# First two projection units piece by piece over the tokens, transposes of x between their k steps, in a retention and attention layer

## The reference, cut to what matters

```python
def _rms_norm(x, g):
    x32 = x.astype(jnp.float32)
    y = x32 * lax.rsqrt(jnp.mean(x32 * x32, axis=-1, keepdims=True) + RMS_EPS)
    return (y * g.astype(jnp.float32)).astype(x.dtype)

hn = _rms_norm(x, norm_mix[l])
proj = hn @ w_in
rq, rk, rv, rg, aq, ak, av, gr, ga = jnp.split(proj, ...)
```

## Time and profile before

| what | us |
|---|---|
| median of three runs | 1802.99 |
| the profiled execution | 1802.53 |
| its span, first to last instruction | 1800.6 |
| TensorE busy | 1769.1 |
| POOL, VectorE, ScalarE busy | 882.4, 765.8, 473.3 |

### The profile page before, as it was taken

One profiled execution on the slowest core, in us unless ns is written; L12 is line 12 of the kernel. 1 busy time (PEld: TensorE's weight loads), 2 busy tenths in 40 slices (PEclk: granted clock), 3 DMA queues, 4 the chain that ended last, 5 costly groups with the idle time before them and its releaser, 6 DMA issues.

```text
span 1800.6 us, 29667 instructions
## 1 busy us (share of the span) xinstructions
PE 1769.1 (98%) x12218; PEld 1729.1 (96%) x12218; DVE 765.8 (43%) x813; ACT 473.3 (26%) x879; POOL 882.4 (49%) x450
## 2 busy tenths in 40 slices
PE   7999999999999999999899998999999999999998
PEld 6999999999999999999899998999999999999998
DVE  4143444443222213314845678455444444632313
ACT  5001010100411125447101125433333333201003
POOL 3323232324333333332336448988888887344550
PEclk9999999999999999999999999999999999999999
DMA  6212121224222252452834342222222221723122
GB/s 241 83 57 64 57 63 58 66 92 152 82 84 90 76 177 88 150 180 75 236 86 144 126 141 83 71 70 70 92 95 70 93 70 50 291 91 122 53 63 95
DMA packets 172694, 186.64 MB, mean 104 GB/s; under 512 B 7353, under 2 KB 149937, under 8 KB 172633
## 3 DMA queue, kind: packets, MB, share of 16 engines
q1 hardware_dynamic: 143088, 136.87, 23.7%
q10 hardware_dynamic: 29545, 48.90, 7.9%
HBM read 131.99 MB, written 53.76 MB: 103 GB/s over the span
## 4 chain that ended last, share of the span: by engine, by line
PE 92%; DVE 4%; ACT 1%; issue 1%; POOL 1%; DMA 0%; ACTq 0%; DVEq 0%; SPq 0%
PE unit_ps L896 55%; PE pair_ps L1232 23%; PE unit_ps L1302 4%; PE task_banks L1081 2%; PE task_banks L1058 1%; PE task_banks L1068 1%; PE task_banks L1008 1%; PE task_banks L985 1%; PE task_banks L992 1%; PE task_banks L994 1%; PE task_banks L1043 0%; PE task_banks L980 0%; PE task_banks L1016 0%; PE task_banks L965 0%; DVE parts L2184 0%
## 5 line engine op out<-in xcount | busy, mean ns | idle before, releaser
L896 PE MATMUL unit_ps<-a_hi,w_part 128*128 128x344 f32 x3552 | 716.5, 327 | 4.7 <-DVE a_lo L1860 3.7
L896 PEld LDWEIGHTS unit_ps<-a_hi,w_part 128*128 128x128 f32 x3552 | 578.5, 189 | 14.8 <-issue 10.6
L776 POOL TENSOR_TENSOR w_part<-w_raw,consts 128x1024 fp32r<-128x1024 f32 (+1 forms) x89 | 212.2, 2384 | 735.1 <-PE unit_ps L896 705.4
L896 PE MATMUL unit_ps<-a_lo,w_part 128*128 128x344 f32 x1776 | 377.3, 321 | 0.0
L896 PEld LDWEIGHTS unit_ps<-a_lo,w_part 128*128 128x128 f32 x1776 | 300.6, 189 | 0.0
L778 POOL TENSOR_TENSOR w_part<-w_raw,w_part 128x1024 fp32r<-128x1024 f32 (+1 forms) x91 | 240.5, 2643 | 7.0
L1232 PE MATMUL pair_ps<-a_hi,slots_a 128*128 128x258 f32 x1056 | 178.4, 283 | 3.4 <-DVE a_lo L2256 1.5
L1232 PEld LDWEIGHTS pair_ps<-a_hi,slots_a 128*128 128x128 f32 x1056 | 148.8, 190 | 4.5 <-DVE a_lo L2256 1.8
L1835 DVE TENSOR_TENSOR stage<-unit_ps,rstd 128x1032 f32<-128x1032 f32 x42 | 51.7, 1231 | 206.4 <-PE unit_ps L896 206.4
L896 PE MATMUL unit_ps<-b_hi,w_part 128*128 128x344 f32 x720 | 133.4, 320 | 0.0
L896 PEld LDWEIGHTS unit_ps<-b_hi,w_part 128*128 128x128 f32 x720 | 117.0, 188 | 0.3 <-DVE gate_a L2218 0.3
(11 more groups left out here) (266 smaller groups left out, 2677.6 us busy)
## 6 DMA issues: line engine op xcount, KB each, us to landing
w_raw<-in_w_in SPq DMA_DIRECT2D x58, 512.0 KB, 3.9
h_spill<-h_out SPq DMA_DIRECT2D x11, 1032.0 KB, 4.9
raw_a<-in_w_gate_up SPq DMA_DIRECT2D x11, 1024.0 KB, 6.9
raw_b<-in_w_gate_up SPq DMA_DIRECT2D x11, 1024.0 KB, 5.1
att_spill<-stage ACTq DMA_DIRECT2D x18, 516.0 KB, 2.7
att_in<-att_spill ACTq DMA_DIRECT2D x3, 3072.0 KB, 11.5
gate_spill<-stage ACTq DMA_DIRECT2D x16, 516.0 KB, 3.5
a_lo<-h_spill SPq DMA_DIRECT2D x15, 516.0 KB, 5.7
```

The source lines that it names most:

```text
L776: pool.tensor_tensor(part[:, 0], raw, one, ALU.mult).then_inc(w_high, 1)
L896: mm = pe.matmul(unit_ps[s][:, n, 0:PIECE], w_part[:, slot, w, k0 + by * k, :], x[:, k, n * PIECE:(n + 1) * PIECE], start=(k == 0 and part ...
```

## The change

- `x_row` becomes nine buffers with a semaphore each, put behind the rows that `v_t` and its neighbours take; no x load waits for a buffer.
- SyncE loads the weights of units 0 and 1 first, then all of x, then the weights of units 2 and 3.
- TensorE turns tiles 0 to 2, then works on units 0 and 1 by piece of 344 tokens: piece 0 of unit 0, piece 0 of unit 1, piece 1 of unit 0, and so on. Tiles 3 to 8 are turned ahead of six of the k steps (`X_TURN`). `unit_done` counts for both units only in the last piece. The norm tasks move from unit 1 to unit 2, the first ahead of its first k step.
- ScalarE and VectorE follow one list, `X_STEPS`: emptying the banks of a tile, and the high or low parts of four k tiles of one piece (344 tokens instead of 1032; 24 passes instead of 8 on each engine).
- On ScalarE the nine squares stand behind the whole list, and the roots behind them.
- VectorE copies units 0 and 1 from their banks unscaled and multiplies them by `rstd` in place later.

```diff
-X_ROWS = 4
+X_TURN = {(0, 0, 3): 3, (0, 1, 0): 4, (0, 1, 4): 5, (1, 0, 1): 6, (1, 0, 5): 7, (1, 1, 1): 8}
+
+X_STEPS = (("turn", 0), ("turn", 1), ("turn", 2), ("rows", 0, 0), ("turn", 3), ("rows", 0, 4), ("turn", 4), ("turn", 5),
+           ("rows", 1, 0), ("turn", 6), ("rows", 1, 4), ("turn", 7), ("turn", 8), ("rows", 2, 0), ("rows", 2, 4))
...
@@ sync
+            for j in range(2):
+                load(Place(0), j, KT, w_in[:, :, cols[j]:cols[j] + P])
             for t in range(CHUNKS + 1):
-                r = t % X_ROWS
-                if t >= X_ROWS:
-
-                    sp.wait_ge(task_done[1], t - X_ROWS + 1)
-                    sp.wait_ge(squared, t - X_ROWS + 1)
...
-                if t == X_ROWS:
-                    load(Place(0), 0, KT, w_in[:, :, cols[0]:cols[0] + P])
-            for j in range(1, 4):
+            for j in range(2, 4):
                 load(Place(0), j, KT, w_in[:, :, cols[j]:cols[j] + P])
...
@@ tensor
-            unit(Place(0), 0, KT, a_hi, a_lo, ready=(a_ready, 0))
-            unit(Place(0), 1, KT, a_hi, a_lo, between=lambda k: x_norm(k) if k < len(X_NORM) else None)
-            for j in range(2, 4):
-                unit(Place(0), j, KT, a_hi, a_lo)
+            for t in range(3):
+                turn_x(t)
+            for n in range(PIECES):
+                for j in range(2):
+                    pe.wait_ge(w_split, j + 1)
+                    c = slice(n * PIECE, (n + 1) * PIECE)
+                    for k in range(KT):
+                        if (n, j, k) in X_TURN:
+                            turn_x(X_TURN[n, j, k])
+                        if n < PIECES - 1:
+                            pe.wait_ge(a_early, n * KT + k + 1)
+                        else:
+                            pe.wait_ge(a_ready, k + 1)
+                        for part, (w, x) in enumerate(((0, a_hi), (0, a_lo), (1, a_hi))):
+                            mm = pe.matmul(unit_ps[j][:, n, 0:PIECE], w_part[:, j, w, k, :], x[:, k, c],
+                                           start=(k == 0 and part == 0), stop=(k == KT - 1 and part == 2))
+                    if n == PIECES - 1:
+                        mm.then_inc(unit_done, 1)
+
+            unit(Place(0), 2, KT, a_hi, a_lo, between=lambda k: x_norm(k) if k < len(X_NORM) else None)
+            unit(Place(0), 3, KT, a_hi, a_lo)
...
@@ scalar
+            def rows_high(n, k0):
+
+                for b in range(2):
+                    act.wait_ge(task_free[b], 3 * (n + 1))
+                c = slice(n * PIECE, (n + 1) * PIECE)
+                for k in range(k0, k0 + 4):
+                    act.activation(a_hi[:, k, c], wide[:, k, c], ACT.Copy, scale=gains[:, 0, k:k + 1])\
+                       .then_inc(a_early_high if n < PIECES - 1 else a_high, 1)
+
+            act.wait_ge(gains_loaded, 16)
+            for step, *at in X_STEPS:
+                if step == "turn":
+                    turned(*at)
+                else:
+                    rows_high(*at)
             for t in range(CHUNKS + 1):
                 n = P if t < CHUNKS else SAMPLES
...
                 wait(act, squared, t)
...
                    .then_inc(squared, 1)
-                turned(t)
-
-            for b in range(2):
-                act.wait_ge(task_free[b], CHUNKS + 1)
-            act.wait_ge(gains_loaded, 16)
-            for k in range(KT):
-                act.activation(a_hi[:, k, :], wide[:, k, :], ACT.Copy, scale=gains[:, 0, k:k + 1]).then_inc(a_high, 1)
...
@@ vector
+            for what, *at in X_STEPS:
+                if what == "turn":
+                    turned(*at)
+                else:
+                    rows_low(*at)
+
+            def unscaled(j):
+                dve.tensor_copy(pieces(v_t[:, j, :]), take(Place(0), j)).then_inc(unit_free[j], 1)
+
+            unscaled(0)
             dve.wait_ge(x_root, 2)
...
+            unscaled(1)
             for b in range(2):
                 dve.wait_ge(task_free[b], T_RET // 2)
-
-            scaled(Place(0), 0, v_t[:, 0, :])
-            scaled(Place(0), 1, v_t[:, 1, :])
+            for j in range(2):
+                dve.wait_ge(unit_free[j], 1)
+                step(dve.tensor_tensor(v_t[:, j, :], v_t[:, j, :], rstd[:], ALU.mult))
```

More of the change, by code:

```diff
@@ L273, in build @@
         with ExitStack() as s:
-            x_row = sb("x_row", [P, X_ROWS, D], stack=s)
+            sb("skipped_x", [P, 7 * TOKENS], stack=s)
+            x_row = sb("x_row", [P, CHUNKS + 1, D], stack=s)
             x_square = sb("x_square", [P, D], stack=s)
@@ L387, in build @@
         table_loaded = sem("table_loaded")
-        x_loaded = [sem(f"x_loaded{i}") for i in range(X_ROWS)]
+        x_loaded = [sem(f"x_loaded{t}") for t in range(CHUNKS + 1)]
         x_spilled = sem("x_spilled")
@@ L393, in build @@
         diag_ready = sem("diag_ready")
+        a_early_high = sem("a_early_high")
+        a_early = sem("a_early")
         a_high = sem("a_high")
@@ L926, in _, with turn_x @@
             pe.wait_ge(const_loaded, 16)
-            for t in range(CHUNKS + 1):
+            def turn_x(t):
                 rows = P if t < CHUNKS else SAMPLES
-                pe.wait_ge(x_loaded[t % X_ROWS], 16 * (t // X_ROWS + 1))
+                pe.wait_ge(x_loaded[t], 16)
                 for b in range(2):
@@ L933, in _ @@
                         c = (4 * b + q) * P
-                        mm = pe.transpose(ps[:, q * P:q * P + rows], x_row[0:rows, t % X_ROWS, c:c + P], ident[0:rows, 0:rows])
+                        mm = pe.transpose(ps[:, q * P:q * P + rows], x_row[0:rows, t, c:c + P], ident[0:rows, 0:rows])
                     end(mm, b)
@@ L1354, in turned @@
                                      full(Place(0), 2 * t + 1)[:].rearrange("p (q t) -> p q t", q=4)[:, :, 0:n], ACT.Copy), 1)
+            def rows_high(n, k0):
[11 more added lines that the diff above has]
+                    rows_high(*at)
             for t in range(CHUNKS + 1):
                 n = P if t < CHUNKS else SAMPLES
-                act.wait_ge(x_loaded[t % X_ROWS], 16 * (t // X_ROWS + 1))
+                act.wait_ge(x_loaded[t], 16)
                 wait(act, squared, t)
-                act.activation(x_square[0:n, :], x_row[0:n, t % X_ROWS, :], ACT.Square, accum_out=x_factor[0:n, t:t + 1])\
+                act.activation(x_square[0:n, :], x_row[0:n, t, :], ACT.Square, accum_out=x_factor[0:n, t:t + 1])\
                    .then_inc(squared, 1)
-                turned(t)
-            for b in range(2):
-                act.wait_ge(task_free[b], CHUNKS + 1)
-            act.wait_ge(gains_loaded, 16)
-            for k in range(KT):
-                act.activation(a_hi[:, k, :], wide[:, k, :], ACT.Copy, scale=gains[:, 0, k:k + 1]).then_inc(a_high, 1)
             act.wait_ge(squared, CHUNKS + 1)
@@ L1846, in norm_factor, with turned @@
                 dve.reciprocal(own, own).then_inc(rstd_ready, 1)
-            for t in range(CHUNKS + 1):
+            def turned(t):
                 n = P if t < CHUNKS else SAMPLES
@@ L1852, in _, with rows_low @@
                                       full(Place(0), 2 * t)[:].rearrange("p (q t) -> p q t", q=4)[:, :, 0:n]), 0)
+            def rows_low(n, k0):
+                for b in range(2):
+                    dve.wait_ge(task_free[b], 3 * (n + 1))
+                c = slice(n * PIECE, (n + 1) * PIECE)
+                for k in range(k0, k0 + 4):
+                    if n < PIECES - 1:
+                        dve.wait_ge(a_early_high, n * KT + k + 1)
+                    else:
+                        dve.wait_ge(a_high, k + 1)
+                    dve.scalar_tensor_tensor(out=a_lo[:, k, c], in0=wide[:, k, c], scalar=gains[:, 0, k:k + 1],
+                                             in1=a_hi[:, k, c].bitcast(F32), op0=ALU.mult, op1=ALU.subtract)\
+                       .then_inc(a_early if n < PIECES - 1 else a_ready, 1)
             dve.wait_ge(const_loaded, 16)
             dve.wait_ge(gains_loaded, 16)
[L1856 to L1861, removed]
+            for what, *at in X_STEPS:
+                if what == "turn":
+                    turned(*at)
+                else:
+                    rows_low(*at)
+            def unscaled(j):
+                dve.tensor_copy(pieces(v_t[:, j, :]), take(Place(0), j)).then_inc(unit_free[j], 1)
+            unscaled(0)
             dve.wait_ge(x_root, 2)
```

4 lines of the change are left out of this document (2 added, 2 removed).

## The result

| | us |
|---|---|
| before, median of 5 runs beside it | 1802.93 |
| after, median of 5 runs (1811.04 to 1815.07) | 1813.23 |
| ratio, 95% interval | 1.0059 (1.0048 to 1.0070) |
| the profiled execution after (the slowest of the five) | 1815.07 |

The change makes the kernel slower by 10.3 us. The forecast was 1809.7 us, so 6.7 us slower. The median lies 0.3 us under the upper end of the range (1813.5).

The account below looks back on a forecast made before the run. TensorE, busy 98% of the span, was taken as the bound. Early start, stop, norm matmuls, unit 2 and low clock put unit 2's end at 69.3 against 62.6 us, +6.7 us: 1809.7 us, range 1805.0 to 1813.5.

Parts of the forecast that it names:

- The stop ahead of the norm matmuls: Ahead of unit 2, TensorE stands 7.8 us, from 45.3 us until the diagonals are ready at 53.1 us.
- the stretch from tile 8 to the diagonal: ScalarE and VectorE work after tile 8 is turned: emptying, high parts, nine squares, roots, diagonal; 18.7 us in sum.
- the low clock behind it: After TensorE's stop the granted clock falls as unit 2 restarts, costing 2.7 us; ends 0 and 3.2 us.
- an earlier start: At the head, TensorE starts unit 0 7.4 us sooner, working by pieces while x is still being turned.
- The forecast's own sign: Stated test at the head: the forecast is wrong if unit 0 starts before 14 us or after 18 us.
- The start at 16.1 us: TensorE starts unit 0 at about 16.1 us, with x tile 0 landing at about 8.3 us.
- 1.5 us between the start and tile 8: Allowance for a wait at k step 4 and a low clock, added to 16.8 us; bounds 0 and 3.2 us.
- Taken alone that is a gain of 3.8 us: TensorE is through units 0 and 1 at 45.3 us, against 49.1 us before without the norm factors.
- (1): Rival: the squares' tail stays hidden and the early start wins; -2.7 us, 1800.3 us; chance 0.06.
- (2): Rival: the stop comes, but the clock doesn't fall and nothing slips early; +2.5 us, 1805.5 us; chance 0.11.
- (3): Rival: slower head, late x, full low clock, table load before the squares; +11.2 us, 1814.2 us; 0.13 together with (4).
- (4): Rival: POOL's lock stretches the low parts of piece 0; 1811 us; chance 0.13 together with (3).

Follow-up runs that it names:

- squares_between: Changed kernel with the nine squares put back between ScalarE's other steps instead of behind the list: 1808.60 us.
- squares_short: Changed kernel with the squares still last but each on 64 of 1024 columns (norm factors wrong): 1807.35 us.
- best2_last: Changed kernel with loads, tile turns and pieces reordered and early table load, all nine squares last: 1802.18 us; with four squares between the tiles, 1797.59 us.
- filler: Changed kernel with TensorE turning the identity 60 times while it waits for the diagonal: 1812.98 us.
- norm_unit3: Changed kernel with the norm matmuls between the k steps of unit 3 instead of unit 2, squares still last: 1813.86 us.
- second profile: The changed kernel run once more, unaltered: median 1814.54 us, its profiled execution 1812.28 us.
- table_early: Changed kernel with a one-column ScalarE copy once the gains are there, so the table load comes early: 1813.47 us.
- x_first: Changed kernel with loads ordered x tile 0, weights 0, x 1 and 2, weights 1, rest of x: 1813.65 us.
- best: Changed kernel with x_first, table_early, tile 3 turned earlier, three squares between tiles, pieces reordered, norm matmuls two k steps later: 1802.67 us.

## Where the prediction was right and where it was wrong

**The sign and the mechanism** were right. The stop ahead of the norm matmuls was put at 7.8 us and is 7.84 us; the stretch from tile 8 to the diagonal at 18.7 us and is 58.8 - 40.2 = 18.6 us; the low clock behind it at 2.7 us and is 2.3 us. That the stop fits is no luck: its two terms, this stretch and the 10.9 us of TensorE's work beside it, are both counted from tile 8 and both fit. squares_between, squares_short and best2_last show that the squares cause it, filler that the clock adds about 2 us, norm_unit3 that a later question for the diagonal doesn't help by itself.

**The step that failed is the part "an earlier start"**, in its two terms; unit 2 ends at 74.8 instead of 69.3 us in the first profile, the slowest of its five runs, and at 71.9 us in the second. The forecast's own sign, unit 0 after 18 us, came up in the first.

- *The start at 16.1 us.* It was 18.27 us. Tile 0 landed at 9.2 instead of 8.3 us: in the first 6 us the queues moved 184 GB/s, and I had used the rate of the full queues for the bytes ahead of x. And a table load of 1.28 us stood between the first transposes and the first emptied bank. I had put it into a rival, ahead of the squares; its place is ahead of the first function, which here waits for TensorE (11.24 us), while before it ran at 1.67 us while x was still on its way. table_early puts its cost at the start at 0.9 us. The rest, 0.3 us, lies between the last transpose and the first product (2.16 us for the 1.9 forecast).
- *1.5 us between the start and tile 8.* From the start to the end of tile 8 the forecast had 16.8 us of work and this 1.5 us; 21.9 us were measured, 5.1 us over the work, beyond the bound of 3.2 us as well. The wait at k step 4 is 1.39 us (1.1 forecast), two later waits for low parts 0.7 us (none forecast), the first nine products took 2.7 instead of 1.4 us and tile 3's transposes 1.5 instead of 0.87 us, together 4.1 us; 1.0 us I can't place. The bound took the wait and the slow clock as alternatives where they came one behind the other. The second profile has the start at 17.38 us with no slow products behind it and tile 8 at 37.3 instead of 40.2 us. That is 3.1 us over the work, inside the bound and still twice the 1.5 us, so the term differs from run to run and was too small in both.

**"Taken alone that is a gain of 3.8 us"** fell with these terms. TensorE was through both units at 51.1 us, not 45.3 us, and so 2.0 us later than the 49.1 us of before; in the second profile it was through at 48.2 us, 0.9 us sooner than before. So even without the stop the early start gives between -2.0 and 0.9 us. In squares_between TensorE is through at 51.6 us, 2.5 us later than before, waits 2.1 us for weights and loses 1.8 us to the clock behind that (unit 2 ends at 69.2 us): 6.4 of the 6.6 us by which its unit 2 is later than the 62.6 us of before. Of the 2.5 us the longer wait at k step 4 is the squares' own.

**Rivals.** (1) fell. (2) fell in both its parts: the clock is low after stops of 7.8, 3.3, 2.7 and 2.1 us, and the head did slip. (3), at 1814.2 us, was the nearest in size: x came late (by 0.9, not 1.5 us), a table load was in the way (at the start, not ahead of the squares), and the slow clock came early. (4), the shared port in piece 0, didn't happen in the changed kernel, whose last split for unit 1 ended at 15.6 us, but decided x_first.

**Nothing else costs**: the later store of x, tables and weights held up no one in the changed kernel, as forecast, and the weights of unit 2 were ready 1.25 us after unit 1 (filler), for 1.1 us forecast, inside the stop. The load behind the norm had some 5 us to spare there, and none once the norm moved (norm_unit3).

## What to carry to other kernels

Work that is taken off the front of an in-order engine's program goes to its end, and its whole length is then compared with what is left on the bound engine: count from the last common event (here tile 8) on both engines, and put such work into the engine's idle stretches instead. An earlier start is worth only what no wait behind it takes back; three edits that each began sooner or waited less gave 0, 0 and 4 us alone, and together with the squares moved, the pieces reordered and the loads and tiles in a third order they turned +10.3 us into -5.1 us. An idle stretch is free only if nothing behind it on the same engine is waited for: three squares ahead of a bank's emptying cost a wait of 2.8 us in squares_between. A short stop of TensorE has to be priced with the low clock behind it, about 2 us here.

## What the runs showed of the hardware that I had not expected

- A stop as short as 2.1 us was followed by a granted clock of 0.57 over 4 us (squares_between), while the 2.16 us ahead of the first unit, the same in the two profiles of the changed kernel, stand between slow transposes and slow products in one (0.24 and 0.29 us apart) and between fast transposes and fast products in the other (0.14 and 0.16 us). In squares_between, with slow transposes, fast products follow. So the stop of 2.16 us by itself doesn't show what the products behind it will do.
- The first table load had two places. It ran at 1.67 us in the kernel before and in best, ahead of its function's wait for a transfer, and at 11.24 us in the changed kernel, where it was itself held until TensorE's first transposes. Why it stands behind the wait there wasn't tested. Between the load and the root that needs it the row shows nothing (55.38 + 1.28 us, root at 56.67 us). The Trainium skill, "ScalarE: Activation LUTs", section "What ACT_TABLE_LOAD costs", adds a drain of about 1.38 us to a switch; in this tail, where it would have lengthened the stop, it isn't there.
- The same program began its first unit at either spacing of products, 0.29 or 0.16 us, in two executions. The Trainium skill, "TensorE: Matmul & The Clock Gate", section "Part 1: The HAM clock gate (the "warmup" mystery)", says that how many matmuls run slow at a kernel's start differs from run to run; the two traces agree.
- VectorE's diagonal held up POOL's split by 0.9 us (squares_between), and POOL's split stretched four low parts from 2.04 to 4.49 us (x_first) and a VectorE step of 8x8 elements from 0.22 to 2.14 us (squares_short): the two hold each other up, and a tiny instruction can pay for a whole split.
